# A hybrid decoder step: joint attention with masks and exponentials issued one unit earlier, and a first output weight with split buffers of its own

## The chip, the cores and the metric

The kernel runs on 1 core of a Trainium2 chip. A core has five engines with an instruction stream each: TensorE (PE: matrix products and transposes), VectorE (DVE), ScalarE (ACT), GpSimd (POOL) and SyncE (SP), which here only issues transfers. They meet through semaphores alone: an instruction that waits holds up everything behind it on its own engine. The metric is the device time of one execution in microseconds. Before the change the median of 3 runs is 2309.22 us (2308.1 to 2314.87).

## The reference

One decoder layer for a prompt of 512 tokens and for 8 samples of 4 new tokens each, which share the weights:

```python
xn = rms_norm(x, norm_mix_w)
aq, ak, av, bq, bk, bv, bz, bb, ba = split(xn @ w_in)
# A: 8 heads x 64; three dilated windows, each a masked softmax, merged by their denominators;
#    a sample reads its cached keys and values as well
a_out = merge_branches(...)
# B: 4 heads, gated delta rule with a 128x128 state per head
b_out = rms_norm(gated_delta_rule(...)) * silu(bz)
h = x + concat([a_out, b_out]) @ w_out
y = h + peer(rms_norm(h))      # 16384 single-neuron experts, 8 heads, 16 picked for each
```

The change lies in branch A and in the first piece of `w_out`.

## The kernel before

The stages follow each other on one core: input projections (to 278 us of the trace), joint attention (278 to 464), delta rule (464 to 687), output projection with the start of the feed-forward part (687 to 763), then routing and the experts, to the end.

**Joint attention** (the `..._attend` functions). The prompt's attention is cut into 32 units: unit u is one query tile i of 128 queries and one head, with (i+1) x 128 keys, so units grow from 128 to 512 columns. Four units make a block b with slots k = 0 to 3, two blocks a query tile, and each block also carries the attention of one sample over its 896 cached rows. One unit passes through:

- PE `scores(u)` (L492, into one of two score banks, `twin`), issued two units ahead,
- DVE `mask(u)` (L634, L637): adds the mask and takes the maximum,
- ACT `exponentials(u)` (L712),
- DVE `norm` (L685, L686): divides by the sum and releases `s_norm`,
- PE `turn(u)` (L501): transposes the probabilities,
- ACT `turned(u)` (L702): evicts them to `pt`,
- PE `values(u)` (L511), into one bank that two units share,
- ACT `pair` (L707): evicts the finished pair to `cat` and frees that bank (`s_cat`).

PE's order in slot k is: the slot's sample part, `turn(u)`, `values(u-1)`, `scores(u+2)`, and a second sample part. The sample parts: the four `turn_keys` (L524, L529) stand in slots 0 and 1, two in each; ACT (`kt_lo`, L719) and DVE (`kt_hi`, L643) evict their two banks. `sample_scores(b)` (L541 to L545) ends slot 2. On DVE `sample_mask(b)` (L655 to L659) stands in slot 3. ACT's `sample_exp` (L724) is in the next block's slot 0, DVE's `sample_norm` (L664, L665) in its slot 1, PE's `turn_sample` (L558) in slot 2, ACT's `sample_turned` (L736 to L738) there too, and PE's `sample_values` (L570) in slot 3. DVE's `own_heads` (L672, `ob`) reads their result in slot 3 and releases `s_kept`. PE's `fold_heads` (L582) stands first in the slot 0 after that; it waits for `s_kept` and for the `masked` that `sample_mask` raises. The whole order is the order of the code; no planner moves it.

**Output weights.** Weights come in pieces; for a product in three passes each is split into a rounded part (`w_hi`, ACT, L1188, `split_weights`) and the rest (`w_lo`, POOL, L1573). Piece 14 (`NW1`) is the first of the output projection, and its raw form has a buffer of its own (`w_first`), loaded early; its two halves go to the buffers of even pieces. In the delta rule the last group of heads, the samples' (`w, s = NB * NL, 0`), ends with ACT's `vnt` copies (L1005) and POOL's scaling of the states (L1149, `ss0`). After it ACT splits `cat` into `cat_hi` (L1353), DVE takes `cat_lo` (L1441), PE multiplies (L2241 to L2243), and SP loads `X` (L1204) once `cat_lo` is done; DVE adds the products to it (L1450).

Of the kernel before, what the change touches and what calls it, by code (L numbers as in the profile page):

```python
# [26 lines left out]
ALU = mybir.AluOpType  # L27
# [140 lines left out]
def hybrid_step(nc, x_p, x_s, kc, vc, conv_state, s0, nmix, win, wg8, qkw, convw, alog, dtb, dnw, wout, nffn,  # L168
                wpq, skt, eu, eu_rows, ev, pos_t, lnc_p, lnc_s, squares,
                y_p, y_s, k_p, v_p, conv_out, s_p, k_s, v_s, s_s, gates_dram, acts_dram):  # L170
    with ExitStack() as ctx:
# [6 lines left out]
        def at(name, offset, shape, dt=F32):  # L178

            size = int(np.prod(shape[1:])) * 4  # L180
            top[0] = max(top[0], offset + size)
            assert offset + size <= 212800, name
            return nc.alloc_sbuf_tensor_at(name, shape, dt, offset=base + offset)
# [105 lines left out]
        own_half, fold = seat_t[:, 0:P], seat_t[:, P:]  # L289
        assert put.pos[0] <= R_STAT + 160 + NT * 64 + 3 * CH * 32  # L290
        w_first = at("w_first", R_E, [P, CH, WC])


        cat_hi = at("cat_hi", R_AQ, [P, CH, TOK], F32R)
# [321 lines left out]
        def dve_attend(dve, chain):  # L616
# [54 lines left out]
                dve.wait_ge(small_in, 16 * 10)  # L671
                nc.vector.tensor_tensor(out=ob[:], in0=value_out, in1=own_half, op=ALU.mult).then_inc(s_kept, 1)  # L672

            mask(0)
            for u in range(len(UNITS)):
                b, k = divmod(u, SLOTS_B)
                if k in (1, 2):
                    keys(b, 2 * k - 1)
                if u + 1 < len(UNITS):
                    mask(u + 1)  # L680
                if k in (0, 1):
                    keys(b, 2 * k)
                n = (UNITS[u][0] + 1) * P
                dve.wait_ge(s_exp, u + 1)
                chain.link(nc.vector.reciprocal(smax[:, u % 4, 3:4], smax[:, u % 4, 2:3]))  # L685
                nc.vector.tensor_scalar(sm[:, u % 4, 0:n], sm[:, u % 4, 0:n], smax[:, u % 4, 3:4], None, ALU.mult).then_inc(s_norm, 1)  # L686
                if k == 1 and b:
                    sample_norm(b - 1)
                if k == 3:
                    sample_mask(b)  # L690
                    if b:
                        own_heads(b - 1)
# [3 lines left out]
        def act_attend(act, chain):  # L696
# [47 lines left out]
                                     folded.rearrange("p (i l) -> p i l", l=NL), ACT.Copy).then_inc(sa["os"], 1)  # L744

            exponentials(0)
            for u in range(len(UNITS)):
                b, k = divmod(u, SLOTS_B)
                if k in (1, 2):
                    keys(b, 2 * k - 1)  # L750
                if u >= 3 and u % 2:
                    pair(u // 2 - 1)
                if u:
                    turned(u - 1)
                if k == 0 and b >= 2:
                    keep_heads(b - 2)
                if k in (0, 1):
                    keys(b, 2 * k)
                if u + 1 < len(UNITS):
                    exponentials(u + 1)  # L760
                if k == 0 and b:
                    sample_exp(b - 1)
                if k == 2 and b:
                    sample_turned(b - 1)
            turned(len(UNITS) - 1)
            pair(len(UNITS) // 2 - 1)
            keep_heads(NB - 2)
            sample_exp(NB - 1)
# [188 lines left out]
        def act_delta(act, chain):  # L957
            act.wait_ge(l2_done, 2 * BH + 1)
            for group in GROUPS:
# [38 lines left out]
                if group[0] < NT - 1:  # L998
                    for n in group:
                        act.wait_ge(dl["os"], n + 1)  # L1000
                        nc.scalar.activation(yv[n % 2][:], quad(1), ACT.Copy).then_inc(dl["o"], 1)
                else:
                    w, s = NB * NL, 0
                    act.wait_ge(dl["s_dve"], 1)
                    nc.scalar.activation(vnt[:, 1].rearrange("p h (b l) -> p h b l", l=NL), sample_bank[:, :, :, 1, :], ACT.Copy)\  # L1005
                        .then_inc(dl["s_act"], 1)
                    act.wait_ge(dl["s_pe"], 2)
                    nc.scalar.activation(ml[s][0:w], quad(2)[0:w], ACT.Copy).then_inc(dl["s_act"], 1)
                    act.wait_ge(dl["s_pe"], 4)
                    nc.scalar.activation(yv[s][0:w], quad(4)[0:w], ACT.Copy).then_inc(dl["o"], 1)  # L1010
# [110 lines left out]
        def pool_mix(pool, chain):  # L1121
# [3 lines left out]
            for group in GROUPS:  # L1125
# [12 lines left out]
                for lv, n in level_steps(group):  # L1138
# [3 lines left out]
                    else:  # L1142
                        pool.wait_ge(dl["y"], step_no[lv - 1, n] + 1)
                    nc.gpsimd.tensor_tensor(out=sub(ml[s], w), in0=sub(lt[s], w), in1=bc(sq[0:w, LEVEL0 + lv, 0:w], 1, BH),
                                            op=ALU.mult).then_inc(dl["ml"], 1)

            pool.wait_ge(dl["s_pe"], 1)
            for h in range(BH):
                tt(out=ss0[:, :, h, :], in0=ss0[:, :, h, :], in1=bc(eg[0][:, h, NL - 1:NB * NL:NL], 2, BD), op=ALU.mult).then_inc(dl["sd"], 1)  # L1149
# [35 lines left out]
        def split_weights(act, k):  # L1185
            act.wait_ge(w_in[k % 2], 16 * (k // 2 + 1))
            act.wait_ge(w_used, k - 1)
            nc.scalar.activation(w_hi[:, k % 2], raw(k)[:], ACT.Copy).then_inc(w_hi_ready, 1)  # L1188

        def raw(k):  # L1190
            return w_first if k == NW1 else w_raw[k % 2]

        def sp_ffn(sp):
            for k in range(NW1 + 2, NW3):
                sp.wait_ge(w_hi_ready, k - 1)
                sp.wait_ge(w_lo_ready, k - 1)
                src = wout[k - NW1] if k < NW2 else wpq[k - NW2]
                sp.dma_start(w_raw[k % 2][:], src).then_inc(w_in[k % 2], 16)
                if k == NW1 + 2:

                    sp.wait_ge(ff["cat_lo"], CAT_PARTS)
                    for t in range(NT):
                        x = x_p[t * P:(t + 1) * P, :] if t < NT - 1 else x_s
                        sp.dma_start(X[0:TILES[t][1], t, :], x).then_inc(x_in[t], 16)  # L1204
                    sp.dma_start(nmix_b[:], nffn.partition_broadcast(P)).then_inc(consts_in, 16)
# [28 lines left out]
        def pe_ffn(pe, product):  # L1234
            pe.wait_ge(dl["cat"], NT)
            uses = 0
            for k in range(NW1, NW2):
                pe.wait_ge(w_lo_ready, k + 1)
                for t in range(NT):
                    if uses >= 4:  # L1240
                        pe.wait_ge(ff["h_used"], uses - 3)
                    tok = token_columns(t)

                    pe.wait_ge(ff["cat_lo"], -(-tok.stop // CAT_COLS))
                    product(bank[2 + uses % 4][:, 0:WC],
                            [(cat_hi[:, c, tok], cat_lo[:, c, tok], w_hi[:, k % 2, c, :], w_lo[:, k % 2, c, :])
                             for c in range(CH)]).then_inc(proj_ready, 1)
                    uses += 1
                pe.wait_ge(proj_ready, READY1 + uses)
                pe.sem_inc(w_used, 1)  # L1250
# [94 lines left out]
            pe_dense(pe, product)  # L1345

        def act_ffn(act, chain):
            split_weights(act, NW1)
            act.wait_ge(dl["cat"], NT)
            act.wait_ge(kv_out, 16 * (NKV + 1))  # L1350
            for i in range(CAT_PARTS):
                cols = slice(i * CAT_COLS, (i + 1) * CAT_COLS)
                nc.scalar.activation(cat_hi[:, :, cols], cat[:, :, cols], ACT.Copy).then_inc(ff["cat_hi"], 1)  # L1353

            for k in range(NW1 + 1, NW2 + 1):
                split_weights(act, k)
            for t, (t0, w) in enumerate(TILES):
                act.wait_ge(ff["h_used"], (NW_OUT - 1) * NT + t + 1)
# [208 lines left out]

        def pool_ffn(pool, chain):
            pool.wait_ge(kv_out, 16 * (NKV + 2))
            for k in range(NW1, NW3):  # L1570
                pool.wait_ge(w_hi_ready, k + 1)
                pool.wait_ge(w_used, k - 1)
                nc.gpsimd.tensor_tensor(out=w_lo[:, k % 2], in0=raw(k)[:], in1=w_hi[:, k % 2].bitcast(F32),  # L1573
                                        op=ALU.subtract).then_inc(w_lo_ready, 1)
            pool.sem_inc(ff["gate_mm"], HOT)
            for s in range(2):
                pool.sem_inc(gate_out[s], 16)
# [819 lines left out]
```

## Time and profile before

| | |
|---|---|
| median of 3 runs | 2309.22 us |
| the profiled execution itself | 2308.13 us |
| its span | 2306.3 us |
| PE busy | 2050.8 us (89%) |
| DVE busy | 1583.5 us (69%) |
| POOL busy | 1159.3 us (50%) |
| ACT busy | 771.7 us (33%) |
| joint attention, 277.7 to 464 | PE busy 151.25 of 186.3 us, granted clock 0.86 |
| delta rule, 464 to 687 | PE busy 166.98 of 223 us, granted clock 0.80 |
| output projection, 687 to 763 | PE busy 61.46 of 76 us, granted clock 0.89 |

Busy time is time in which an engine executes; the granted clock is TensorE's, 1.00 being 2.4 GHz and 0.50 being 1.2 GHz. A wait in brackets at a row's end is idle time just before that instruction, with what ended it.

### The profile page before, as it was taken

Reading aid. Unit: us, or ns where it says so; the run is one execution under the profiler, and the core shown is the slowest. Engines: PE = TensorE matmul, PEld = TensorE weight load, DVE = VectorE, ACT = ScalarE, POOL = GpSimd, SP = SyncE. Lnnn points to the kernel's source line nnn. Section 1 sums busy time; section 2 is a strip of 40 time slices with the busy share of each in tenths; the row PEclk is TensorE's granted clock in tenths of the full one; section 3 lists DMA queues with packets and bytes.
Section 4 is the critical chain, followed back from the end, with each engine's and each line's share of the span. In section 5 each row is a group of like instructions: output and inputs, shape, how many; then the busy total and the mean of one; then the engine's idle time right before and its main releaser. Section 6 shows DMA issues by size and latency. Waiting matters only on the chain.

```text
span 2306.3 us, 34698 instructions
## 1 busy us (share of the span) xinstructions
PE 2050.8 (89%) x12706; PEld 1908.5 (83%) x12706; DVE 1583.5 (69%) x3094; ACT 771.7 (33%) x1228; POOL 1159.3 (50%) x632
## 2 busy tenths in 40 slices
PE   5999878786768897999998888889989999999998
PEld 5989744575748896998888887889979999999998
DVE  2478443344433202779986999994469999999996
ACT  3223133323221323444444334333323333333332
POOL 2336000031113232477676343437788888888884
PEclk9999787988958898999999999999989999999999
DMA  5664354243523254477778567769979998999894
GB/s 183 214 224 158 133 160 160 66 164 156 190 76 122 85 230 166 145 243 225 233 236 272 214 237 263 257 239 367 364 273 315 320 318 309 309 319 313 313 325 139
DMA packets 176598, 520.95 MB, mean 226 GB/s; under 512 B 15153, under 2 KB 86065, under 8 KB 170705
## 3 DMA queue, kind: packets, MB, share of 16 engines
q1 hardware_dynamic: 136560, 290.94, 36.7%
q0 software_dynamic: 36864, 134.23, 17.5%
q10 hardware_dynamic: 3056, 94.24, 10.7%
q8 instruction: 70, 1.15, 0.2%
q14 instruction: 48, 0.39, 0.1%
HBM read 456.81 MB, written 128.49 MB: 254 GB/s over the span
## 4 chain that ended last, share of the span: by engine, by line
DVE 42%; PE 40%; issue 6%; POOL 4%; DMA 4%; ACT 4%; SPq 0%; ACTq 0%; DVEq 0%; PEldq 0%; POOLq 0%
DVE acc_g L1883 10%; DVE act_l L1867 9%; PE bank L2241 6%; PE bank L2242 6%; PE bank L2243 6%; DVE one L1561 6%; DVE one L1560 5%; DVE rows_g L1731 3%; POOL u_lo L1706 3%; PE twin L2241 2%; PE twin L2243 2%; PE twin L2242 2%; PE twin L492 1%; PE bank L511 1%; DMA w_raw<-wpq 1%
## 5 line engine op out<-in xcount | busy, mean ns | idle before, releaser
L1706 POOL TENSOR_TENSOR u_lo<-u_raw,u_hi 128x1024 fp32r<-128x1024 f32 x128 | 316.4, 2472 | 330.4 <-ACT u_hi L1686 329.8
L2241 PE MATMUL bank<-hn_hi,u_hi 128*128 128x416 f32 x1024 | 374.6, 366 | 33.4 <-POOL u_lo L1706 32.5
L1911 POOL TENSOR_TENSOR v_lo<-v_raw,v_hi 128x1024 fp32r<-128x1024 f32 x128 | 336.6, 2631 | 70.4 <-ACT v_hi L1836 69.2
L2242 PE MATMUL bank<-hn_lo,u_hi 128*128 128x416 f32 x1024 | 363.6, 355 | 0.0
L2243 PE MATMUL bank<-hn_hi,u_lo 128*128 128x416 f32 x1024 | 362.1, 354 | 0.0
L1883 DVE SCALAR_TENSOR_TENSOR acc_g<-rows_g,coef,acc_g 128x1024 f32<-128x1024 f32 x127 | 289.9, 2282 | 17.1 <-DMA rows_g<-ev,idx_g 16.6
L2242 PE MATMUL bank<-a_lo,v_hi 128*128 128x416 f32 x768 | 269.1, 350 | 0.0
L2241 PE MATMUL bank<-a_hi,v_hi 128*128 128x416 f32 x768 | 269.1, 350 | 0.0
L2243 PE MATMUL bank<-a_hi,v_lo 128*128 128x416 f32 x768 | 269.0, 350 | 0.0
L2241 PEld LDWEIGHTS bank<-hn_hi,u_hi 128*128 128x128 f32 x1024 | 196.0, 191 | 49.1 <-POOL u_lo L1706 46.3
L1867 DVE TENSOR_TENSOR act_l<-act_l,gin 128x416 f32<-128x416 f32 x128 | 229.2, 1791 | 0.6 <-DMA act_l<-acts_dram 0.5
L1731 DVE CUSTOM_DVE_ANT_0 rows_g<-rows_g,twin 128x1024 f32<-128x1024 f32 x128 | 154.9, 1210 | 91.6 <-DMA rows_g<-eu_rows,idx_g 91.2
L1838 ACT ACTIVATE a_hi<-act_l 128x416 fp32r<-128x416 f32 x128 | 70.7, 552 | 378.9 <-DVE act_l L1867 378.9
L2243 PEld LDWEIGHTS bank<-hn_hi,u_lo 128*128 128x128 f32 x1024 | 195.0, 190 | 2.4
L2242 PEld LDWEIGHTS bank<-hn_lo,u_hi 128*128 128x128 f32 x1024 | 195.4, 191 | 1.0
L1721 POOL DMA_INDIRECT rows_g<-ev,idx_g x128 | 180.2, 1408 | 20.9 <-issue 14.8
L1702 ACT ACTIVATE act_c<-bank 128x416 f32<-128x416 f32 x128 | 66.3, 518 | 347.9 <-PE bank L2243 339.7
L1561 DVE TENSOR_SCALAR one<-bank,picks_t 128x128 f32<-128x128 f32 x416 | 162.5, 391 | 0.0
L1337 PE MATMUL bank<-one,one 128*128 128x128 f32 x832 | 117.1, 285 | 39.3 <-DVE one L1561 38.0
L1337 PEld LDWEIGHTS bank<-one,one 128*128 128x128 f32 x832 | 105.3, 194 | 54.2 <-DVE one L1561 52.9
L2243 PEld LDWEIGHTS bank<-a_hi,v_lo 128*128 128x128 f32 x768 | 144.2, 188 | 1.1
L2242 PEld LDWEIGHTS bank<-a_lo,v_hi 128*128 128x128 f32 x768 | 144.2, 188 | 1.1
(414 smaller groups left out, 4629.3 us busy)
## 6 DMA issues: line engine op xcount, KB each, us to landing
u_raw<-eu SPq DMA_DIRECT2D x128, 512.0 KB, 4.9
v_raw<-ev SPq DMA_DIRECT2D x128, 512.0 KB, 4.7
k_s<-kc ACTq DMA_DIRECT2D x29, 1104.0 KB
v_s<-vc ACTq DMA_DIRECT2D x29, 1104.0 KB
acts_dram<-act_c SPq DMA_DIRECT2D x128, 208.0 KB, 3.9
gates_dram<-gst ACTq DMA_DIRECT2D x8, 3328.0 KB, 12.3
gin<-gates_dram SPq DMA_DIRECT2D x32, 832.0 KB, 8.1
act_l<-acts_dram SPq DMA_DIRECT2D x64, 416.0 KB, 5.6
```

What stands on the lines that cost most here:

```text
L1337: last = nc.tensor.matmul(quad(4 + n % 2)[:, j, :], one2[n % HOT][:, j, :], one1[n % HOT][:, j, :], start=True, stop=True)
L1560: ts(one2[n % HOT][:, j, :], asc_p, picks_t[:, 1, c:c + 1], None, ALU.is_equal)
L1561: last = ts(one1[n % HOT][:, j, :], asc_p, picks_t[:, 0, c:c + 1], picks_t[:, 2, c:c + 1], ALU.is_equal, ALU.mult)
L1706: nc.gpsimd.tensor_tensor(out=u_lo[s][:], in0=u_raw[2 * (x % 2) + s][:], in1=u_hi[s][:].bitcast(F32), op=ALU.subtract).then_inc(dn["ulo"], 1)
L1721: nc.gpsimd.indirect_dma_start(out=rows_g[ROW_AT[m]][0:NG, :], out_offset=None, in_=table, in_offset=bass.IndirectOffsetOnAxis(ap=idx_g[0: ...
L1731: nc.vector.tensor_tensor_reduce(out=row, in0=row, in1=x_held[0:NG, :], scale=1.0, scalar=0.0, op0=ALU.mult, op1=ALU.add, accum_out=pre_g[ ...
L1867: tt(out=a.rearrange("p (b t) -> p b t", b=GBLOCKS), in0=a.rearrange("p (b t) -> p b t", b=GBLOCKS), in1=gin[f // 4 % 2][:, :, f % 4, :], ...
L1883: nc.vector.scalar_tensor_tensor(out=acc_g[0:NG], in0=rows_g[ROW_AT[m]][0:NG, :], scalar=coef[0:NG, n:n + 1], in1=acc_g[0:NG] if n else xg ...
L1911: nc.gpsimd.tensor_tensor(out=v_lo[f % 4][:], in0=v_raw[f % 4][:], in1=v_hi[f % 4][:].bitcast(F32), op=ALU.subtract).then_inc(dn["vlo"], 1)
L2241: nc.tensor.matmul(out, ah, bh, start=first and i == 0, stop=False)
L2242: nc.tensor.matmul(out, ah, bl, start=False, stop=False)
L2243: last = nc.tensor.matmul(out, al, bh, start=False, stop=final and i == n - 1)
```

## The change

DVE's and ACT's orders in the joint attention are written anew: masks and exponentials run two units ahead, not one, DVE normalises unit u+1 in slot u, and the evictions of keys move within the slots. PE's and SP's orders stay. For the first output weight there are two buffers of its own (`first_hi`, `first_lo`, in a region that the attention has left); its split moves from the output stage into the delta rule, on ACT ahead of the `vnt` copy of the last group, on POOL ahead of the state scaling. SP waits for the whole `cat` before it loads piece 16.

```diff
+        first_hi = at("first_hi", R_QK, [P, CH, WC], F32R)
+        first_lo = at("first_lo", R_QK + 8192, [P, CH, WC], F32R)
...
-            mask(0)
-            for u in range(len(UNITS)):
-                b, k = divmod(u, SLOTS_B)
-                if k in (1, 2):
-                    keys(b, 2 * k - 1)
-                if u + 1 < len(UNITS):
-                    mask(u + 1)
-                if k in (0, 1):
-                    keys(b, 2 * k)
+            def norm(u):
                 n = (UNITS[u][0] + 1) * P
                 dve.wait_ge(s_exp, u + 1)
...
+            mask(0)
+            mask(1)
+            norm(0)
+            for u in range(len(UNITS)):
+                b, k = divmod(u, SLOTS_B)
+                if k in (0, 1):
+                    keys(b, 2 * k)
+                if u + 1 < len(UNITS):
+                    norm(u + 1)
+                if u + 2 < len(UNITS):
+                    mask(u + 2)
+                if k in (0, 1):
+                    keys(b, 2 * k + 1)
                 if k == 1 and b:
                     sample_norm(b - 1)
                 if k == 3:
...
             exponentials(0)
+            exponentials(1)
             for u in range(len(UNITS)):
                 b, k = divmod(u, SLOTS_B)
-                if k in (1, 2):
-                    keys(b, 2 * k - 1)
-                if u >= 3 and u % 2:
-                    pair(u // 2 - 1)
-                if u:
-                    turned(u - 1)
                 if k == 0 and b >= 2:
                     keep_heads(b - 2)
                 if k in (0, 1):
                     keys(b, 2 * k)
-                if u + 1 < len(UNITS):
-                    exponentials(u + 1)
+                if k == 2 and b:
+                    sample_turned(b - 1)
+                if u >= 3 and u % 2:
+                    pair(u // 2 - 1)
+                turned(u)
+                if k in (0, 1):
+                    keys(b, 2 * k + 1)
+                if u + 2 < len(UNITS):
+                    exponentials(u + 2)
                 if k == 0 and b:
                     sample_exp(b - 1)
-                if k == 2 and b:
-                    sample_turned(b - 1)
-            turned(len(UNITS) - 1)
...
                     w, s = NB * NL, 0
+                    split_weights(act, NW1)
                     act.wait_ge(dl["s_dve"], 1)
...
+            split_lo_weights(pool, NW1)
             pool.wait_ge(dl["s_pe"], 1)
...
         def sp_ffn(sp):
+            sp.wait_ge(dl["cat"], NT)
             for k in range(NW1 + 2, NW3):
...
-            split_weights(act, NW1)
             act.wait_ge(dl["cat"], NT)
             act.wait_ge(kv_out, 16 * (NKV + 1))
+            split_weights(act, NW1 + 1)
```

On DVE, at the end of a block of 512-column units (slot 3, then the next block's slot 0), there stood before, with `sss` the sample's probabilities, `ob` what `own_heads` writes, and L634 the mask:

```order
L686 TENSOR_SCALAR sm<-sm,smax 128x512 [waits dve_chain]
L655 ISA sss_139,sstat<-bank,lncs 128x512 [waits sample_turned,sample_scores]
L655 ISA sstat 128x1
L655 ISA sss_139,sstat<-bank,lncs 128x384
L655 ISA sstat 128x1
L655 ISA sss_139,sstat<-bank,lncs 128x32
L655 ISA sstat 128x1
L659 TENSOR_REDUCE sstat<-sstat 128x1 [waits dve_chain]
L672 TENSOR_TENSOR ob<-bank,seat_t 128x128 [waits small_in,l2_rt,sample_out]
L634 ISA sm,smax<-twin,lncp 128x512 [waits s_turned,s_scores]
L634 ISA smax 128x1
L637 TENSOR_SCALAR smax<-smax 128x1 [waits dve_chain]
```

At the same place there stands now (L636 is the mask, L657 to L661 the sample mask, L674 `own_heads`, L645 `keys`):

```order
L636 ISA sm,smax<-twin,lncp 128x512 [waits s_turned,s_scores]
L636 ISA smax 128x1
L639 TENSOR_SCALAR smax<-smax 128x1 [waits dve_chain]
L657 ISA sss_139,sstat<-bank,lncs 128x512 [waits sample_turned,sample_scores]
L657 ISA sstat 128x1
L657 ISA sss_139,sstat<-bank,lncs 128x384
L657 ISA sstat 128x1
L657 ISA sss_139,sstat<-bank,lncs 128x32
L657 ISA sstat 128x1
L661 TENSOR_REDUCE sstat<-sstat 128x1 [waits dve_chain]
L674 TENSOR_TENSOR ob<-bank,seat_t 128x128 [waits small_in,l2_rt,sample_out]
L645 COPY kt_hi<-bank 128x384 [waits sample_kt1,sample_scores]
```

The mask of the second unit of the next block now stands ahead of the sample mask and `own_heads`, where it stood behind both.

On ACT, in slots 0 and 1 of a block of 384-column units, there stood before (L743 is `keep_heads`, L719 the keys, L712 the exponentials, L724 the sample exponentials, L707 the pair, L702 `turned`):

```order
L743 ACTIVATE cat<-bank 128x4x4 [waits l2_rt]
L719 ACTIVATE kt_lo<-bank 128x512 [waits sample_kt0,sample_scores]
L712 ACTIVATE sm,smax<-sm,smax 128x384 [waits s_masked]
L724 ACTIVATE sss_139,sstat<-sss_139,sstat 128x928 [waits sample_masked]
L719 ACTIVATE kt_lo<-bank 128x512 [waits sample_kt0,sample_scores]
L707 ACTIVATE cat<-bank 128x128 [waits s_out]
L702 ACTIVATE pt<-bank 128x384 [waits s_out,s_turned]
```

and there stands now (in the same sequence L751, L727, L720, L732, L715 and L710):

```order
L751 ACTIVATE cat<-bank 128x4x4 [waits l2_rt]
L727 ACTIVATE kt_lo<-bank 128x512 [waits sample_kt0,sample_scores]
L710 ACTIVATE pt<-bank 128x384 [waits s_out,s_turned]
L727 ACTIVATE kt_lo<-bank 128x512 [waits sample_kt0,sample_scores]
L720 ACTIVATE sm,smax<-sm,smax 128x384 [waits s_masked]
L732 ACTIVATE sss_139,sstat<-sss_139,sstat 128x928 [waits sample_masked]
L727 ACTIVATE kt_lo<-bank 128x512 [waits sample_kt0,sample_scores]
L715 ACTIVATE cat<-bank 128x128 [waits s_out]
L710 ACTIVATE pt<-bank 128x384 [waits s_out,s_turned]
```

The exponentials here are those of one unit later, and they stand behind `turned` and a second eviction of keys; the pair is still behind the sample exponentials and one eviction of keys.

On POOL, at the end of the delta rule, there stood before (`ss` the states, `w_first` the raw first output weight):

```order
L1144 TENSOR_TENSOR ml_118<-lt_102,sq 32x4x32 [waits delta_x0]
L1149 TENSOR_TENSOR ss_131<-ss_131,eg_98 128x8x128 [waits delta_s_pe]
L1149 TENSOR_TENSOR ss_131<-ss_131,eg_98 128x8x128 x3
L1573 TENSOR_TENSOR w_lo<-w_first,w_hi 128x2048 [waits w_used,w_hi_ready,kv_out]
L1573 TENSOR_TENSOR w_lo<-w_raw_81,w_hi 128x2048 [waits w_used,w_hi_ready]
```

and there stands now:

```order
L1152 TENSOR_TENSOR ml_118<-lt_102,sq 32x4x32 [waits delta_x0]
L1202 TENSOR_TENSOR first_lo<-w_first,first_hi 128x2048 [waits w_used,w_hi_ready]
L1158 TENSOR_TENSOR ss_131<-ss_131,eg_98 128x8x128 [waits delta_s_pe]
L1158 TENSOR_TENSOR ss_131<-ss_131,eg_98 128x8x128 x3
L1202 TENSOR_TENSOR w_lo<-w_raw_81,w_hi 128x2048 [waits w_used,w_hi_ready,kv_out]
```

The first weight's rest moved ahead of the state scaling, and the wait for the caches' write (`kv_out`) is now that of the second weight.

## Rows read from the trace of the kernel before

**Rows 1.** Windows by block, from fold to fold; columns as in the header.

```profile
core 0: us, PE busy (x) PEld busy (x) DVE busy (x) ACT busy (x) POOL busy (x), PEclk, DMA share, GB/s
334.52:360.04 25.52, 21.60 (x161) 12.49 (x160) 8.73 (x34) 8.04 (x24) 0.00 (x0) 0.73 0.46 151
360.04:381.32 21.28, 17.23 (x171) 10.95 (x170) 9.40 (x34) 8.78 (x24) 0.00 (x0) 1.00 0.54 176
381.32:409.17 27.85, 23.77 (x172) 13.86 (x171) 9.53 (x34) 8.89 (x24) 0.00 (x0) 0.75 0.43 136
409.17:432.82 23.65, 19.46 (x182) 12.26 (x182) 10.19 (x34) 9.53 (x24) 0.00 (x0) 1.00 0.27 83
```

**Rows 2.** PE's waits in the attention stage: us in total, times, longest.

```profile
PE bank L501 <- DVE sm L686: 20.7, 17, 1.4
PE bank L558 <- DVE kt_hi L643: 5.7, 7, 0.8
```

**Rows 3.** PE timeline, block from 432.82: start us, us, instruction, idle before.

```profile
432.82 0.40 PE L582 MATMUL bank<-seat_t,ob 128*128 128x16 f32 x2
...
436.94 1.12 PE L492 MATMUL twin<-qkt 64*128 64x512 f32 x2
...
441.69 0.66 PE L501 MATMUL bank<-sq,sm 128*128 128x128 f32 x4 [1.31 <-DVE sm L686]
```

**Rows 4.** DVE timeline, from the sample mask to the next block's first mask.

```profile
428.07 0.69 DVE L655 CUSTOM_DVE_ANT_0 sss<-bank,lncs 128x512 f32<-128x512 f32 x1 [0.26 <-PE bank L545]
...
429.92 0.29 DVE L672 TENSOR_TENSOR ob<-bank,seat_t 128x128 f32<-128x128 f32 x1 [0.37 <-PE bank L570]
432.93 0.69 DVE L634 CUSTOM_DVE_ANT_0 sm<-twin,lncp 128x512 f32<-128x512 f32 x1 [2.71 <-PE twin L492]
...
433.66 0.15 DVE L637 TENSOR_SCALAR smax<-smax 128x1 f32<-128x1 f32 x1
```

**Rows 5.** ACT timeline, slots 0 and 1 of the same block.

```profile
434.29 0.71 ACT L712 ACTIVATE sm<-sm,smax 128x512 f32<-128x512 f32 x1
...
434.99 1.06 ACT L724 ACTIVATE sss<-sss,sstat 128x928 f32<-128x928 f32 x1
...
438.74 0.60 ACT L719 ACTIVATE kt_lo<-bank 128x512 f32<-128x512 f32 x1 [2.60 <-PE bank L524]
439.24 0.27 ACT L707 ACTIVATE cat<-bank 128x128 f32<-128x128 f32 x1
```

**Rows 6.** PE timeline: the wait ahead of a fall of the clock.

```profile
389.52 0.55 PE L501 MATMUL bank<-sq,sm 128*128 128x128 f32 x3 [1.24 <-DVE sm L686]
```

**Rows 7.** Windows: that fall; an undisturbed block up to its sample values.

```profile
390.40:403.90 13.50, 12.69 (x46) 6.62 (x48) 3.02 (x11) 3.64 (x11) 0.00 (x0) 0.50 0.41 136
...
360.04:376.85 16.81, 13.09 (x95) 8.18 (x98) 7.66 (x26) 8.27 (x23) 0.00 (x0) 1.00 0.55 173
```

**Rows 8.** PE timeline: the longest wait at the stage's end.

```profile
457.99 1.26 PE L558 MATMUL bank<-sq,sss 128*128 128x128 f32 x7 [2.26 <-DVE sss L665]
```

**Rows 9.** Windows: just after that wait; around a wait among the experts.

```profile
458.60:461.90 3.30, 2.69 (x37) 1.51 (x38) 0.00 (x0) 0.48 (x3) 0.00 (x0) 0.50 0.02 5
...
1204.50:1214.50 10.00, 7.45 (x41) 7.01 (x40) 7.34 (x24) 4.83 (x6) 7.20 (x5) 1.00 0.72 247
```

**Rows 10.** Timeline, end of the delta rule to the output projection.

```profile
659.94 1.91 POOL L1149 TENSOR_TENSOR ss<-ss,eg 128x1024 f32<-128x1024 f32 x1 [21.28 <-PE bank L934]
...
660.22 0.28 ACT L1005 ACTIVATE vnt<-bank 128x128 f32<-128x128 f32 x1 [14.28 <-DVE vnt L1082]
...
689.80 1.29 DVE L1441 TENSOR_TENSOR cat_lo<-cat,cat_hi 128x1088 fp32r<-128x1088 f32 x1 [3.83 <-ACT cat_hi L1353]
691.21 5.45 POOL L1573 TENSOR_TENSOR w_lo<-w_first,w_hi 128x2048 fp32r<-128x2048 f32 x1 [22.77 <-DMA s_s<-ss]
...
697.74 5.66 DVE L1441 TENSOR_TENSOR cat_lo<-cat,cat_hi 128x1088 fp32r<-128x1088 f32 x1
...
712.71 0.75 DVE L1450 TENSOR_TENSOR X<-X,twin 128x256 f32<-128x256 f32 x2 [9.32 <-DMA X<-x_s]
...
713.19 0.39 PE L2241 MATMUL twin<-w_hi,cat_hi 128*128 128x256 f32 x1 [2.95 <-DVE X L1450]
```

More of the change, by code:

```diff
@@ L1187, in split_weights, with split_lo_weights, hi, lo @@
             act.wait_ge(w_used, k - 1)
-            nc.scalar.activation(w_hi[:, k % 2], raw(k)[:], ACT.Copy).then_inc(w_hi_ready, 1)
+            nc.scalar.activation(hi(k), raw(k)[:], ACT.Copy).then_inc(w_hi_ready, 1)
+        def split_lo_weights(pool, k):
+            pool.wait_ge(w_hi_ready, k + 1)
+            pool.wait_ge(w_used, k - 1)
+            nc.gpsimd.tensor_tensor(out=lo(k), in0=raw(k)[:], in1=hi(k).bitcast(F32), op=ALU.subtract).then_inc(w_lo_ready, 1)
         def raw(k):
             return w_first if k == NW1 else w_raw[k % 2]
+        def hi(k):
+            return first_hi[:] if k == NW1 else w_hi[:, k % 2]
+        def lo(k):
+            return first_lo[:] if k == NW1 else w_lo[:, k % 2]
         def sp_ffn(sp):
+            sp.wait_ge(dl["cat"], NT)
             for k in range(NW1 + 2, NW3):
@@ L1245, in pe_ffn @@
                     product(bank[2 + uses % 4][:, 0:WC],
-                            [(cat_hi[:, c, tok], cat_lo[:, c, tok], w_hi[:, k % 2, c, :], w_lo[:, k % 2, c, :])
+                            [(cat_hi[:, c, tok], cat_lo[:, c, tok], hi(k)[:, c, :], lo(k)[:, c, :])
                              for c in range(CH)]).then_inc(proj_ready, 1)
@@ L1353, in act_ffn @@
                 nc.scalar.activation(cat_hi[:, :, cols], cat[:, :, cols], ACT.Copy).then_inc(ff["cat_hi"], 1)
-            for k in range(NW1 + 1, NW2 + 1):
+            for k in range(NW1 + 2, NW2 + 1):
                 split_weights(act, k)
@@ L1569, in pool_ffn @@
             pool.wait_ge(kv_out, 16 * (NKV + 2))
[L1570 to L1574, printed above, removed]
+            for k in range(NW1 + 1, NW3):
+                split_lo_weights(pool, k)
             pool.sem_inc(ff["gate_mm"], HOT)
```

## The prediction

> **What bounds the kernel now.** I read the busy table first, then the blocks of the attention stage as windows, PE's list of waits there, three timelines (PE, DVE, ACT) of one block, the granted clock around the stage's longest waits, and last the timeline at the start of the output projection.
>
> In the attention stage PE runs in the order of its code, and a block's length is PE's work, PE's waits and TensorE's clock. In the blocks from 360.04 and 409.17 PE is busy for 17.23 of 21.28 and 19.46 of 23.65 us, at a clock of 1.00 [rows 1]. Almost all else is waits with a partner. The first is what the change is aimed at: `turn(u)` waits for DVE's normalised probabilities, 17 times, 20.7 us in all, about 1.22 each [rows 2]. The reader should see in PE's timeline that this happens in slots 0 and 1 of each block, where the key evictions stand between a mask and its norm on DVE: 1.31 us before the transposes at 441.69 [rows 3].
>
> The other thing to see is the clock. Of the four blocks shown two are at 1.00 and two at 0.73 and 0.75, and these two last longer [rows 1]. In the block from 381.32 the stretch 390.40 to 403.90 stood at 0.50, which is 1.2 GHz, and it began right after `turn` had waited 1.24 us at 389.52 [rows 6, 7]. The block lasts 27.85 us, and the mean of the undisturbed ones on both sides is (21.28 + 23.65) / 2 = 22.47: the fall cost 5.4 us. The block from 334.52 has the same pattern, so the stage holds two such falls, 10.8 us.
>
> **The change, part by part.** The profiled execution took 2308.13 us for a span of 2306.3, and the median of the runs shown, 2309.22, stands 1.1 above it; I sum against the execution and add the 1.1 at the end.
>
> *Removed: the waits of `turn`.* With mask and exponentials a unit further ahead, `norm(u)` is done a slot before PE wants it. I take all 20.7 us away [rows 2]. PE then comes sooner to what stands behind these waits, and three things there become late.
>
> *Added: the fold waits.* DVE's slot 3 now holds the mask of unit u+2 ahead of `sample_mask` and `own_heads`. That mask needs the scores that PE issues last in slot 3, and PE's next instruction, the fold of the next block, needs what these two write. Today `own_heads` is done at 430.21, and the fold at 432.82 follows the scores without a wait [rows 3, 4]. In the new order, from the same point: the mask starts at 432.93 and lasts to 433.81 (0.88); `sample_mask` lasts from 428.07 to 429.55, where DVE's idle 0.37 us before 429.92 begins (1.48); `own_heads` lasts 0.29 [rows 4]. That is 433.81 + 1.48 + 0.29 = 435.58 less some tenth that neighbours overlap, so 2.6 us after 432.82. In blocks with narrower units the mask is shorter; I take 2.5 as the mean. Six folds stand in the loop (blocks 2 to 7): 15.0 us. What is queued behind on DVE is the key eviction and the norm of slot 0, both needed only after the fold. The bounds are 6 x 2.0 and 6 x 2.8.
>
> *Added: `values` in slot 1.* On ACT the pair's eviction that frees the bank of `values` still stands behind the sample exponentials and a key eviction, and the exponentials ahead of them now wait for the mask of the scores just issued. Scores at 436.94 end at 438.06 [rows 3]; the mask takes 0.99 to its end (0.11 to start, 0.88), the exponentials 0.71, the sample exponentials 1.06, the key eviction 0.50 (to the next start at 439.24) and the pair 0.27 [rows 4, 5]: 441.6. Without its wait PE would reach the transposes at 441.69 - 1.31 = 440.38, and `values` about 0.6 later, at 441.0 [rows 3]. With some 0.3 for four handovers between engines that is 0.9 a block, for 7 blocks 6.3; the bounds are 0 and 1.3 each, the upper one what `turn` waits now.
>
> *Added to an existing wait: `turn_sample` in slot 2.* It waits 0.81 now, for a key eviction on DVE, 5.7 in 7 blocks [rows 2]. Now `sample_norm` stands behind the mask and an eviction, and both before and after it needs the late sample exponentials. I estimate 0.75 more for each, as long as the mask that it is put behind (0.88) less the overlap: 5.2, bounds 0 and 7 x 0.88 = 6.2.
>
> At an unchanged clock the attention gives -20.7 + 15.0 + 6.3 + 5.2 = +5.8. The waits are no fewer; they are moved and joined into longer ones.
>
> *The clock.* This decides. The trace shows which waits the clock outlasts. After 2.26 us before `turn_sample` at 457.99 it was 0.50 [rows 8, 9]. Among the experts PE idles for 10.00 - 7.45 = 2.55 us of a window at 1.00 and keeps it; there PE has worked without a break ahead [rows 9]. In the attention, with its many short waits, 1.24 us sufficed once [rows 6]. So of two waits like the new 2.6 one was followed by a fall and one was not, and the fold's place is nearer in kind to the first. I take 4 of the 6 folds to be followed by one.
>
> How long does it last? The falls of today ended only when PE was in the sample scores and values, whose stream has no wait in it; the one shown ended at 403.90 [rows 7]. From the fold at 360.04 to the sample values at 376.85 PE has 13.09 us of work [rows 7]. I let the fall begin 0.7 later and hide the new 0.9 of `values`: 13.09 - 0.7 - 0.9 = 11.5 us more a fall. The lower bound is that a fall costs what today's did, 5.4. The two falls of today lie behind waits of `turn` that go, so they go too: -10.8. With 4 falls: 4 x 11.5 - 10.8 = +35.2.
>
> The Trainium skill, "TensorE: Matmul & The Clock Gate", section "HAM oscillation — how this bites in real kernels", speaks of an engine that falls back when bursts are parted by waits for a transfer, and its example has waits longer than the 2.6 us worked out here. By it the new waits would leave the clock alone; the trace disagrees so far as the fall after 1.24 us goes [rows 6]. The sum would be that of the second rival below.
>
> *The first output weight.* ACT's split (1.90, as its like) goes ahead of the `vnt` copy, before which ACT has been idle for 14.28 us [rows 10]; POOL's difference, 5.45 at 691.21, goes ahead of the state scaling, before which POOL has been idle for 21.28 [rows 10]. Both idle times are the wait for PE's 64 products with the sample states, and the inputs are there long before, so the cost is nothing; if the raw weight were late, up to 5.45 would lie on the path. DVE idles there as well, so nothing beside it is slowed.
>
> In the output stage POOL then has one difference where it had two. DVE's `cat_lo` shows what that is worth: the first piece takes 1.29, the last 5.66, since it runs beside POOL's second difference [rows 10]. So the last ends 5.66 - 1.29 = 4.4 us earlier, and with it the load of `X` that waits for it and lands before 712.71. PE itself can start some 5.5 us earlier, one difference of 5.45, but has to wait for `X`: it does so now for 2.95 us at 713.19 [rows 10]. The gain is that of `X`, 4.4; the bounds are 0, if POOL's second difference moves beside `cat_lo` after all, and 8.8, if both slow pieces are freed. SP's added wait for `cat` comes while nothing that it loads is wanted: 0.
>
> *Sum:* 2308.13 + 5.8 + 35.2 - 4.4 = 2344.7, and with the 1.1 of the median 2345.8.
>
> **The rivals.**
>
> *Falls as short as today's.* At half clock PE has hardly a wait left (12.69 busy of 13.50), which may bring the clock back before the sample scores [rows 7]. Against it: today's lasted to those scores. With 4 falls: 4 x 5.4 = 21.6, less 10.8, gives 2308.13 + 5.8 + 10.8 - 4.4 + 1.1 = 2321.4.
>
> *No more falls than today.* The 2.55 among the experts left the clock at 1.00 [rows 9]. Two falls of the same price elsewhere in the stage: 2308.13 + 5.8 - 4.4 + 1.1 = 2310.6.
>
> *The falls vanish: faster.* The place is slots 0 and 1. Two short waits of `turn` follow each other there in each block, and one of these was followed by the fall at 390.40 [rows 6, 7]; if it is their closeness that brings the clock down and not a single wait's length, the change takes both away and the fold's wait, alone between dense work, does nothing. That decides from no fall at all in blocks 2 to 7: 2310.6 - 10.8 = 2299.8. Against it: the wait at 457.99 stands alone, and the clock was at 0.50 behind it [rows 8, 9].
>
> *The clock doesn't come back.* If a fall lasts past the scores to the next fold, the blocks stay at half: some 17.5 us of work in each of 6, so +105 less the hidden waits of 25 and 10.8: about 2380.
>
> **How the numbers follow.** Falls to the sample scores, 3 to 6 of them (2334 to 2369): 0.50, the forecast. Short falls (2316 to 2332): 0.19. No more than today: 0.15. None: 0.10. Not back: 0.06. A measurement of this kernel tells no less than about 0.3% from nothing, which is 6.9 us, so below 2302.3 is faster and above 2316.1 slower. Faster: the case of no falls, 0.10, with 0.02 for a gain of 8.8 in the output stage beside today's falls: 0.12. Same: the rest of that second rival, 0.13, and 0.02 of the short falls: 0.15. Slower: 0.73. The range for 8 in 10 runs from 2306, within the second rival with a larger gain in the output stage, to 2368; the likeliest case alone has 2334 to 2369.
>
> **What the profile after would show.** PE's waits on the norm of `turn` near 0. At `fold_heads` six waits of 2.4 to 2.8 us, released by DVE's `own_heads` or the sample mask before it. `values` waiting for the pair, 0.5 to 1.3, in seven blocks, and `turn_sample` 1.3 to 1.7 for `sample_norm`. The clock by block: 1.00 in at most three of the blocks 2 to 7, and about 0.65 in the others, from the fold to the sample scores. In the output stage the last `cat_lo` near 1.3 and the landing of `X` 4.4 us earlier after the delta rule. The forecast is wrong if the folds wait but the clock stays at 1.00, or if DVE's slot 3 is through before PE's scores end, so that the fold does not wait at all.

## The result and the profile after

The changed kernel takes 2315.97 us, the median of 20 runs, against 2309.21 us for the kernel before, also of 20: a ratio of 1.0031, interval [1.0017, 1.0045]. That is slower, as forecast, by 6.8 us, and far from the 2345.8 that was forecast: the time stands at the low end of the rival with short falls (2316 to 2332). Single runs of the kernel before lie between 2298.71 and 2326.14 us, those of the changed one between 2310.05 and 2323.35.

PE's waits in the attention stage after (us in total, times, longest) answer to [rows 2]:

```profile
PE bank L584 <- DVE ob L674: 15.9, 7, 2.7
PE bank L560 <- DVE sss L667: 13.0, 8, 2.3
PE twin L494 <- DVEq L628: 4.0, 1, 4.0
PE bank L513 <- ACT cat L715: 2.8, 3, 1.2
PE bank L503 <- PE bank L572: 2.3, 7, 0.3
...
PE bank L526 <- ACT kt_lo L727: 0.4, 1, 0.4
```

The waits of `turn` for the norm are gone, all 20.7 us of them. In their place stand the folds (L584), six of 2.4 to 2.7 us and a last of 0.5 that was there before, `turn_sample` (L560), with 10.7 for seven where it had 5.7 (the eighth, of 2.3, was there before), and `values` (L513), three times.

PE's timeline after, the block from 413.74 and the fold of the next, answers to [rows 3], and DVE's around that fold to [rows 4]:

```profile
422.65 1.06 PE L513 MATMUL bank<-pt,av 128*64 128x128 f32 x8 [1.07 <-ACT cat L715]
...
427.20 1.50 PE L560 MATMUL bank<-sq,sss 128*128 128x128 f32 x7 [1.53 <-DVE sss L667]
...
442.01 0.58 PE L584 MATMUL bank<-seat_t,ob 128*128 128x16 f32 x2 [2.71 <-DVE ob L674]
```

```profile
439.33 0.69 DVE L636 CUSTOM_DVE_ANT_0 sm<-twin,lncp 128x512 f32<-128x512 f32 x1 [4.14 <-PE twin L494]
...
440.18 0.69 DVE L657 CUSTOM_DVE_ANT_0 sss<-bank,lncs 128x512 f32<-128x512 f32 x1
...
441.62 0.29 DVE L674 TENSOR_TENSOR ob<-bank,seat_t 128x128 f32<-128x128 f32 x1
```

Mask, sample mask and `own_heads` follow each other, and the fold starts 0.1 us after the last of them. The fold, 0.40 us long in [rows 3], lasts 0.58: the clock is already down.

The whole stage as one window, from its first scores to its last fold, before and after (columns as in [rows 1]):

```profile
277.72:463.66 185.94, 150.91 (x1319) 93.91 (x1319) 72.12 (x274) 66.56 (x191) 0.00 (x0) 0.86 0.37 120
```

```profile
277.50:476.25 198.75, 162.74 (x1319) 108.10 (x1319) 73.28 (x274) 67.05 (x191) 0.00 (x0) 0.79 0.34 112
```

The stage is 12.8 us longer. PE executes the same 1319 instructions, for 11.8 us more, and it idles 36.0 us where it idled 35.0. So all but 1 us of the loss is clock, not waiting. Blocks after, then the six stretches of half clock behind the folds, and below them two more, behind waits of `turn_sample`:

```profile
336.16:361.90 25.74, 21.09 (x160) 14.13 (x160) 9.13 (x34) 8.24 (x24) 0.00 (x0) 0.75 0.44 143
361.90:386.97 25.07, 19.95 (x169) 13.02 (x170) 9.59 (x34) 8.78 (x24) 0.00 (x0) 0.86 0.46 146
386.97:413.74 26.77, 22.06 (x171) 14.58 (x172) 9.92 (x34) 9.10 (x24) 0.00 (x0) 0.82 0.46 148
413.74:442.01 28.27, 22.20 (x182) 14.76 (x182) 10.39 (x34) 9.63 (x24) 0.00 (x0) 0.86 0.20 67
...
335.40:345.50 10.10, 9.14 (x36) 7.08 (x37) 3.63 (x16) 4.34 (x11) 0.00 (x0) 0.50 0.40 123
362.80:369.30 6.50, 6.39 (x23) 4.25 (x22) 2.32 (x7) 2.64 (x6) 0.00 (x0) 0.50 0.37 134
386.80:396.60 9.80, 9.52 (x37) 7.41 (x37) 2.53 (x9) 3.92 (x10) 0.00 (x0) 0.50 0.32 115
414.10:417.20 3.10, 3.10 (x15) 2.77 (x16) 1.11 (x3) 1.30 (x3) 0.00 (x0) 0.50 0.57 217
441.40:454.70 13.30, 12.59 (x48) 9.72 (x49) 4.11 (x14) 4.97 (x11) 0.00 (x0) 0.50 0.19 72
...
311.60:321.40 9.80, 8.18 (x31) 6.13 (x31) 3.79 (x16) 4.40 (x12) 0.00 (x0) 0.50 0.48 166
...
349.20:352.40 3.20, 3.20 (x14) 2.16 (x14) 0.18 (x1) 0.86 (x4) 0.00 (x0) 0.50 0.88 270
427.70:430.80 3.10, 3.10 (x14) 2.05 (x13) 0.04 (x1) 0.92 (x4) 0.00 (x0) 0.50 0.00 0
```

Each of the six folds has one, which begins in the wait or within 0.9 us of its end, and no block is at 1.00. They last 3 to 13 us, 8.8 in the mean, and the short two come on top, after `turn_sample` has waited 1.53 us. Half of PE's busy time in the six, 48.9 / 2 = 24.5 us or 4.1 for one fall, is what the lower clock cost if everything in them took twice as long.

In the output stage, to set beside [rows 10]:

```profile
656.57 1.91 ACT L1197 ACTIVATE first_hi<-w_first 128x2048 fp32r<-128x2048 f32 x1 [0.18 <-ACT wq L1003]
658.55 4.51 POOL L1202 TENSOR_TENSOR first_lo<-w_first,first_hi 128x2048 fp32r<-128x2048 f32 x1 [9.44 <-ACT first_hi L1197]
...
700.40 1.29 DVE L1462 TENSOR_TENSOR cat_lo<-cat,cat_hi 128x1088 fp32r<-128x1088 f32 x1 [3.97 <-ACT cat_hi L1374]
...
708.39 1.28 DVE L1462 TENSOR_TENSOR cat_lo<-cat,cat_hi 128x1088 fp32r<-128x1088 f32 x1
718.75 0.75 DVE L1471 TENSOR_TENSOR X<-X,twin 128x256 f32<-128x256 f32 x2 [9.09 <-DMA X<-x_s]
```

The early split runs where both engines were idle. The last `cat_lo` takes 1.28 us for 5.66, and from the first `cat_lo` to the addition of `X` 18.35 us pass, where it was 712.71 - 689.80 = 22.91 [rows 10].

### The profile page after: what moved, and what is told of

Read it like the earlier page. It is cut to its first block, busy times and chain, and to the rows that moved or that the text cites. A ratio compares the mean times of both kernels' runs of the same rounds, so it can differ in the third digit from the quotient of the medians.

```text
span 2310.3 us, 34698 instructions
## 1 busy us (share of the span) xinstructions
PE 2055.1 (89%) x12706; PEld 1916.9 (83%) x12706; DVE 1580.2 (68%) x3094; ACT 772.2 (33%) x1228; POOL 1152.9 (50%) x632
## 3 DMA queue, kind: packets, MB, share of 16 engines
q10 hardware_dynamic: 3056, 94.24, 10.7%
## 4 chain that ended last, share of the span: by engine, by line
DVE 43%; PE 37%; issue 7%; ACT 4%; DMA 4%; POOL 4%; SPq 0%; ACTq 0%; DVEq 0%; PEldq 0%; POOLq 0%
DVE acc_g L1901 10%; DVE act_l L1885 9%; DVE one L1582 6%; PE bank L2259 6%; PE bank L2260 5%; PE bank L2261 5%; DVE one L1581 5%; DVE rows_g L1749 3%; POOL u_lo L1724 2%; PE twin L2259 2%; DMA w_raw<-wpq 2%; PE twin L2260 2%; PE twin L2261 2%; PE twin L494 1%; PE bank L513 1%
## 5 line engine op out<-in xcount | busy, mean ns | idle before, releaser
L1901 DVE SCALAR_TENSOR_TENSOR acc_g<-rows_g,coef,acc_g 128x1024 f32<-128x1024 f32 x127 | 289.6, 2280 | 18.2 <-DMA rows_g<-ev,idx_g 17.8
L1582 DVE TENSOR_SCALAR one<-bank,picks_t 128x128 f32<-128x128 f32 x416 | 171.3, 412 | 0.0
L1138 POOL TENSOR_TENSOR qd<-co,eg 128x512 f32<-128x512 f32 x4 | 5.1, 1269 | 286.3 <-ACT eg L970 286.3
L1581 DVE TENSOR_SCALAR one<-bank,picks_t 128x128 f32<-128x128 f32 x416 | 146.4, 352 | 0.1
```

Of the source, the lines that this page charges most:

```text
L1581: ts(one2[n % HOT][:, j, :], asc_p, picks_t[:, 1, c:c + 1], None, ALU.is_equal)
L1582: last = ts(one1[n % HOT][:, j, :], asc_p, picks_t[:, 0, c:c + 1], picks_t[:, 2, c:c + 1], ALU.is_equal, ALU.mult)
L1901: nc.vector.scalar_tensor_tensor(out=acc_g[0:NG], in0=rows_g[ROW_AT[m]][0:NG, :], scalar=coef[0:NG, n:n + 1], in1=acc_g[0:NG] if n else xg ...
```

## The experiments

Ratios are to the kernel before in runs on the same chip; its median there moved between 2303 and 2308 us, so the ratios are what compares.

**The two parts apart.** First the new order alone (before, with DVE's and ACT's attention loops of the changed kernel), then the early split alone:

> The new order of DVE and ACT in the attention, with the first output weight split as before. Theory A (the order costs 12.8 us in the attention stage, and the early split gives 4.4 back in the output stage): about 2309 + 12 = 2321 us, the load of X landing as late after the delta rule as in the kernel before, six waits of about 2.6 us at the fold. Rival (the early split does nothing, the 4.4 us of the profiled pair are chance): the same as the changed kernel, 2316.

Measured: 2315.81 us, ratio 1.0054 [1.0032, 1.0075], 12.3 us above the median of before in these runs; theory A had 12. In its profile, too, half clock follows each of the six folds, for 7.4 us in the mean.

> The attention in the old order, the first output weight split early. Theory A: 4.4 us less than before, about 2305 us, with the last piece of cat_lo at 1.3 us. Rival (the gain is eaten at the wait for X or by SP's added wait): 2309, within 0.1%.

Measured: 2303.13 us, ratio 1.0003 [0.9982, 1.0025]; in its profile the last `cat_lo` is as short as after the change. The order alone carries the loss. For the weight these runs don't decide: 4.4 us are 0.2%, which lies within the interval.

**The fold freed.** In the changed kernel:

```diff
                 if u + 1 < len(UNITS):
                     norm(u + 1)
+                if k == 3:
+                    sample_mask(b)
+                    if b:
+                        own_heads(b - 1)
                 if u + 2 < len(UNITS):
                     mask(u + 2)
...
-                if k == 3:
-                    sample_mask(b)
-                    if b:
-                        own_heads(b - 1)
```

> The changed kernel with sample_mask and own_heads put ahead of the mask of unit u+2 in DVE's slot 3. Both theories: no wait at the six folds (15.4 us less). Theory A (the half clock of the stage follows the fold waits): the falls behind the folds, some 4 us each, go with them, while the waits of values and turn_sample come out in full (about +4): 2316 - 15.4 + 4 - 20 = 2285 us. Rival B (falls come and go without regard to the fold waits): only the waits go, 2316 - 15.4 + 4 = 2305 us, and the attention has half clock for as long as now.

Measured: 2278.97 us, ratio 0.9887 [0.9859, 0.9916]. Against the changed kernel's ratio that is 1.44%, 33 us, where the fold waits hold 15.4. Two of its blocks, of the widths of those from 361.90 and 386.97 above:

```profile
343.91:364.13 20.22, 16.86 (x171) 10.99 (x170) 9.58 (x34) 8.43 (x24) 0.00 (x0) 1.00 0.58 187
364.13:384.98 20.85, 17.49 (x172) 11.19 (x171) 9.73 (x34) 8.54 (x24) 0.00 (x0) 1.00 0.55 179
```

The clock is at 1.00 and PE's busy time is 3 to 4.6 us less for the same work. Theory A had 31 us less, rival B 11. What this run can't say is whether the clock followed the idle time or the new order of work; the next pair does.

**The idle time filled, the wait kept.** PE makes transposes that nothing reads, ahead of the fold:

```diff
+            def fill(u, n):
+                if u:
+                    pe.wait_ge(s_pt, u)
+                for _ in range(n):
+                    nc.tensor.transpose(quad(0)[:, 0, :], ident, ident)
...
                     if b >= 2:
+                        fill(u, 14)
                         fold_heads(b - 2)
```

> The changed kernel, and ahead of each of the six fold waits PE makes 14 transposes of a constant into a free bank (about 2.3 us), which nothing reads: the fold is as late as before, but PE works while it waits. Theory A (the idle time of PE at the fold brings the half clock): the clock stays at 1.00 from fold to fold, and the time falls by the cost of the falls, some 4 us each less what then comes out of the hidden waits: about 2316 - 18 = 2298 us. Rival B (the falls don't hang on that idle time): 2316 us or a little more, with half clock as before.

Measured: 2298.02 us, ratio 0.9959 [0.9941, 0.9977].

> As the run with the filled fold, but with 7 transposes, so that about 1.4 us of idle time are left of each fold wait. If the clock falls behind a fold in proportion to its idle time, half of the gain: about 2307 us. If idle time of this length is outlasted, as most waits of turn in the kernel before were, nearly the whole gain: about 2300 us. Rival B: 2316.

Measured: 2299.96 us, ratio 0.9979 [0.9960, 0.9998]. First a fold and the block behind it with 14 transposes, and two of PE's waits in that run; then, with 7, two folds and the stretches of half clock:

```profile
396.95 1.75 PE L590 MATMUL bank<-sq 128*128 128x128 f32 x14
399.73 0.37 PE L584 MATMUL bank<-seat_t,ob 128*128 128x16 f32 x2 [1.04 <-DVE ob L681]
```

```profile
399.73:424.87 25.14, 20.73 (x196) 13.80 (x196) 10.39 (x34) 9.63 (x24) 0.00 (x0) 1.00 0.25 75
```

```profile
PE bank L513 <- ACT cat L722: 7.6, 7, 1.2
...
PE bank L526 <- ACT kt_lo L734: 2.5, 6, 0.4
```

```profile
355.68 0.36 PE L584 MATMUL bank<-seat_t,ob 128*128 128x16 f32 x2 [1.67 <-DVE ob L681]
...
405.37 0.37 PE L584 MATMUL bank<-seat_t,ob 128*128 128x16 f32 x2 [1.80 <-DVE ob L681]
```

```profile
356.40:359.50 3.10, 3.10 (x13) 2.30 (x12) 1.05 (x3) 1.09 (x2) 0.00 (x0) 0.50 0.70 230
380.40:383.50 3.10, 3.10 (x16) 2.77 (x15) 1.05 (x3) 1.27 (x3) 0.00 (x0) 0.50 0.73 258
431.70:434.60 2.90, 2.90 (x14) 2.24 (x12) 1.11 (x3) 0.94 (x2) 0.00 (x0) 0.50 0.36 137
```

The folds are no earlier in PE's order and wait for the same instruction, and PE only does useless work meanwhile; that alone gives back 0.72%, 17 us; the intervals of the two ratios leave 11 to 22. The size fits the rows: 24.5 us of the six falls, less the waits that half clock had hidden and that come out now (`values` 7.6 for 2.8, key evictions 2.5 for 0.4), are 17.6. The transposes took 0.125 us each and not the 0.165 that I had reckoned with, so 0.7 to 1.0 us stayed idle with 14 and 1.5 to 1.8 with 7. The folds followed by a fall are none of six with 14, three of six with 7, and six of six without a filler. The shorter idle time was outlasted in part, and not by its length alone: 1.67 us at 355.68 was followed by a fall, 1.80 at 405.37 was not. The three falls were short.

**The half clock of the kernel before.** Six transposes ahead of each wait of `turn` in slots 0 and 1 of the kernel before (`if k in (0, 1): fill(u, 6)`):

> The kernel before, with 6 transposes of a constant (about 1 us) ahead of each wait of turn in slots 0 and 1, so that PE works while it waits; no wait is made shorter. If the half clock of the kernel before also follows PE's waits: no fall in its blocks 2 to 7, some 10 us less in the profile of before, and a smaller spread from run to run. If those falls have another cause: the time of before.

Measured: 2287.91 us, ratio 0.9936 [0.9914, 0.9957]. From 309.79 on all six blocks stand at 1.00, and single runs lie within 9.7 us. One of the blocks, and PE's wait there:

```profile
391.59:415.26 23.67, 20.76 (x194) 13.56 (x193) 10.20 (x34) 9.53 (x24) 0.00 (x0) 1.00 0.27 85
```

```profile
PE bank L501 <- DVE sm L694: 9.8, 16, 1.4
```

The kernel before also loses some 15 us to the clock, and not the 10.8 of the prediction. Its profile holds a third stretch of half clock that the prediction did not count, at the stage's start:

```profile
277.70:298.10 20.40, 16.81 (x73) 10.18 (x73) 6.69 (x30) 5.69 (x19) 0.00 (x0) 0.50 0.27 88
```

The changed kernel has two shorter ones in the same first two blocks:

```profile
277.50:284.10 6.60, 6.55 (x27) 5.17 (x28) 3.19 (x15) 2.75 (x10) 0.00 (x0) 0.50 0.00 0
297.90:308.00 10.10, 9.33 (x74) 4.77 (x78) 2.17 (x8) 1.52 (x7) 0.00 (x0) 0.50 0.57 184
```

Half of the busy time is 8.4 us before and 7.9 after, so the change gave almost nothing back there. With the filler two short stretches are left there, of 3.4 and 6.7 us. A second profile of each kernel tells how much of the half clock recurs:

> The kernel before, profiled once more, to see how much of its half clock is the same in another execution. If the falls have fixed places: 342 to 356 and 390 to 404 again, at 13.5 us each. If they are a matter of chance: other places and lengths, and a time that follows them.

> The changed kernel, profiled once more. If the half clock follows the fold waits: a fall at five or six of the six folds again, with other lengths. If chance: falls at places unlike those of the first profile.

2302.43 and 2313.76 us, one run each. A block of each second profile:

```profile
316.44:343.35 26.91, 23.30 (x158) 13.90 (x157) 8.60 (x34) 7.93 (x24) 0.00 (x0) 0.62 0.45 139
```

```profile
338.45:364.20 25.75, 21.10 (x160) 14.13 (x160) 9.13 (x34) 8.24 (x24) 0.00 (x0) 0.75 0.45 148
```

Before, the fall now stands in the block ahead of those of [rows 1], which lasted 18.98 us at 1.00 in the first profile, and the two falls of [rows 1] are gone: in blocks 2 to 7 they change place from run to run. After, the block from 336.16 recurs within 0.01 us, and four others within 0.02: behind the long waits the falls came at the same places both times.

**How long a fall lasts.** The kernel before, with the fold made late and the waits of `turn` kept:

```diff
                 if u + 1 < len(UNITS):
                     mask(u + 1)
+                if k == 0 and b:
+                    sample_mask(b - 1)
+                    if b > 1:
+                        own_heads(b - 2)
                 if k in (0, 1):
...
-                if k == 3:
+                if k == 3 and b == NB - 1:
                     sample_mask(b)
-                    if b:
-                        own_heads(b - 1)
+                    own_heads(b - 1)
```

> The kernel before with sample_mask and own_heads moved behind the mask in the next block's slot 0, so that the six fold waits of 2.6 us come beside the waits of turn, which stay. Theory C (a fall lasts as long as short waits go on behind it, so the 11.5 us that were predicted for one belong to an order that keeps the waits of turn): the falls behind the folds last 13 us and more, about 2309 + 15 + 6 x 6 = 2360 us. Rival (a fall's length does not hang on those waits): falls as in the changed kernel, 7 us in the mean and 4 us each in price, 2309 + 15 + 20 = 2344 us or less.

Measured: 2346.5 us, ratio 1.0195 [1.0161, 1.0229]. PE's waits, and the stretches of half clock behind the six folds:

```profile
PE bank L501 <- DVE sm L690: 21.5, 17, 1.9
PE bank L582 <- DVE ob L672: 15.4, 6, 2.7
```

```profile
316.80:340.20 23.40, 20.13 (x80) 11.72 (x83) 6.27 (x23) 7.55 (x23) 0.00 (x0) 0.50 0.36 119
347.40:370.90 23.50, 20.23 (x76) 11.62 (x78) 6.41 (x23) 7.47 (x22) 0.00 (x0) 0.50 0.35 117
378.30:388.00 9.70, 8.35 (x31) 5.81 (x31) 2.23 (x7) 3.67 (x10) 0.00 (x0) 0.50 0.32 102
405.60:435.70 30.10, 26.70 (x132) 16.08 (x136) 7.07 (x23) 8.40 (x23) 0.00 (x0) 0.50 0.29 95
443.10:452.80 9.70, 8.28 (x29) 5.32 (x28) 2.19 (x5) 3.60 (x8) 0.00 (x0) 0.50 0.20 72
473.60:483.70 10.10, 8.46 (x29) 5.49 (x28) 2.54 (x8) 4.14 (x10) 0.00 (x0) 0.50 0.15 57
```

The fold waits are the same 15.4 us, and their falls last 17.8 us in the mean, not 8.8; one costs 92.1 / 2 / 6 = 7.7 us, not 4.1. By the ratio the time is 45 us above the kernel before, between theory C (51) and the rival (35 or less); in the length of falls it is nearer to C. But the mean is made of two kinds: three falls of 23 to 30 us, which the changed kernel never has, and three of about 10, which it has too. The two orders differ in PE's waits above all by those of `turn`, so I take these for what can hold the clock down; that is an inference from this pair, since ACT's order differs too, and why three of the six ended early stays open.

**The other waits, and the best version.** On top of the freed fold, `sample_norm` ahead of the mask in DVE's slot 1 and `sample_exp` ahead of the exponentials in ACT's slot 0:

> As the run with the freed fold, and besides sample_exp ahead of the exponentials in ACT's slot 0 and sample_norm ahead of the mask in DVE's slot 1. Theory A: the waits of values go (7 x 0.9) and turn_sample is back at 0.8 (7 x 0.7 less): 11 us less than the run with the freed fold, about 2274 us, at full clock from block 2 on. Rival B: the 11 us as well, but from its higher start, about 2294 us.

Measured: 2270.46 us, ratio 0.9849 [0.9820, 0.9878]. `turn_sample` is back at 5.7 us; `values` still waits, as long as ever, a miss: in slot 0 `sample_exp` stood behind a key eviction that waits for PE. Moved right behind `turned`:

> As the run with all three waits freed, but with sample_exp right behind turned in ACT's slot 0, ahead of the key eviction that there waits for PE. Theory: the pair is then through before PE reaches values, seven waits of 1.07 us go, and turn_sample stays at 0.81: 2270.5 - 7.5 = 2263 us. Rival (the key eviction of slot 1 holds the pair up, not the sample exponentials): the waits of values stay, 2270.

Measured: 2264.43 us, ratio 0.9822 [0.9801, 0.9843]. PE's waits for the pair in the two runs:

```profile
PE bank L513 <- ACT cat L715: 7.5, 7, 1.1
```

```profile
PE bank L513 <- ACT cat L715: 3.0, 7, 0.6
```

The waits shrink and don't vanish, and the ratio falls by 0.27%, 6 us of the 7.5 expected. This one beats the kernel before by 1.8% and the changed one by 2.1%. With its scatter small, the weight can be weighed:

> The attention of the run with sample_exp first, the first output weight split as in the kernel before. If the 4.4 us that the output stage gains in the profiles reach the end: 4.4 more than that run, about 2267 us. If they are lost again later: the same as that run.

Measured: 2268.78 us, ratio 0.9838 [0.9818, 0.9858], in the same set of runs: 4.35 us more. The five runs of each hardly overlap (2260.41 to 2267.12 against 2266.39 to 2274.33), so the early split's gain reaches the end; that it is all of the 4.4 us they can't say to the microsecond.

## Why the prediction was wrong

- *Waits of `turn` removed, 20.7:* right, all are gone.
- *Fold waits, 15.0:* right, 15.4 at six folds, released by `own_heads`.
- *`values`, 0.9 each:* right in size (1.07), but only three of seven show up, since half clock hides the rest; 7.5 us at full clock, for 6.3 forecast.
- *`turn_sample` 0.75 more each:* right, 1.53 where 0.81 + 0.75 = 1.56 was forecast.
- *Early split, -4.4:* right, 4.56 less from `cat_lo` to `X` in the profile, 4.35 between the medians of the last two runs.
- *Falls behind the folds, 4 of 6:* too few, it is 6 of 6 in both profiles, and in that of the order alone.
- *Price of a fall, 11.5:* wrong, and this is the step that failed. "The falls of today ended only when PE was in the sample scores and values" rested on one execution of an order with two waits of `turn` in every block. The change takes those away, and each fall behind a fold then ended in slot 0 or 1, ahead of `turn_sample`, after 8.8 us in the mean, at 4.1 us; the six blocks stood at 0.75 to 0.86, where 0.65 was forecast for those hit. With the waits of `turn` kept one costs 7.7, so as far as that pair of runs goes I took the removed waits off the sum and left them in the price. The rival with short falls came nearest: in it the clock comes back before the sample scores, at 5.4 each.
- *The falls of today, 10.8:* too little. The same profile has the stretch from 277.70 besides, half of whose busy time is 8.4 us, the filled kernel before shows some 15 us in all, and in blocks 2 to 7 the place moves from run to run.
- *What the clock hides:* while PE is slow, `values` (2.8 us shown for 6.3 in the sum) and the key evictions (0.4 for 2.9) hardly wait, 6.0 us that the sum did not take off.

In sum, 5.8 were forecast for waits and 35.2 for the clock; measured are 1.0 in PE's idle time (5.8 - 6.0 is -0.2) and 11.8 in its busy time. The direction came out right by the clock alone, with more falls than forecast at a third of the price. In the profiled pair -4.4 in the output stage, -2.1 in the delta rule and -2.3 after it leave a span 4.0 longer, within the scatter of the 6.8 that the medians show.

The rival "no more falls than today", by which waits of 2.6 us leave the clock alone, fell with the filled folds: six of six such waits were followed by a fall, and with PE kept busy in them none. The Trainium skill, "TensorE: Matmul & The Clock Gate", section "A second HAM failure mode: psum-queue depth-cycling", says that short idles between groups of products, when they come often enough, can make the clock swing; the runs agree: falls followed idle stretches of 1.2 us [rows 6] to 2.7 us here.

## What to carry to other kernels

Before a stage's waits are moved, ask which of them PE meets as one long idle stretch: here six waits of 2.6 us cost 15 us as waits and some 17 more as clock, though PE's idle time was hardly larger than before. Let the instruction that releases PE's next wait stand ahead of one that itself waits for PE's last product, on every engine; three such swaps are worth 2.1% here. And price a clock fall from the order that will be there, with its waits, not from the one that is removed; a profile of a stage with short waits should be taken twice.

## What the hardware showed

Useless transposes in a wait that stays paid here: 14 ahead of each of six folds gave some 17 us, six ahead of each wait of `turn` some 15 us in the kernel before. The scatter of the kernel before, 2282.66 to 2326.14 us over all its runs, seems to be mostly the clock in this stage: the runs of the filled kernel lie within 9.7 us, those of the best version within 6.7.
